# Closing steps of a threshold search taken between logits, and modulation steps moved to both ends of the attention stage

## What is computed

```python
mod = c_act @ w_ada[l] + b_ada[l]
sh1, sc1, gt1, sh2, sc2, gt2 = jnp.split(mod, 6)      # axis -1
h = rms_norm(x, g_pre_mix) * (1.0 + sc1) + sh1
qa, ka, va, cq, ckv, kidx, widx = split(h @ w_in)
out_a = sliding_window_sink_attention(qa, ka, va, ...)   # window of 2 chunks of 64
# group B, blocks of 128 queries:
score = einsum(w_idx, relu(q_idx . k_idx)); idx = top_k(score, 256)
logits over the kept keys - slopes * distance; softmax; times v
mix = concat(out_a, out_b) @ w_o
x = x + gt1 * rms_norm(mix, g_post_mix)
h2 = rms_norm(x, g_pre_ffn) * (1.0 + sc2) + sh2
x = x + gt2 * rms_norm((silu(gate) * up) @ w_down, g_post_ffn)
```

## Time and profile before

| what | value |
|---|---|
| median of 3 runs | 3391.96 us (3391.65 to 3392.4) |
| profiled execution, its own time | 3388.4 us |
| its span | 3386.6 us |
| TensorE busy over the span | 2987.1 us (88%) |
| VectorE busy | 1701.3 us (50%) |
| ScalarE busy | 1574.6 us (46%) |
| GpSimd busy | 318.4 us (9%) |

### The profile page before, as it was taken

One profiled execution on the slowest core, in us unless ns is written; L12 is line 12 of the kernel. 1 busy time (PEld: TensorE's weight loads), 2 busy tenths in 40 slices (PEclk: granted clock), 3 DMA queues, 4 the chain that ended last, 5 costly groups with the idle time before them and its releaser, 6 DMA issues. The chain is left out here.

```text
span 3386.6 us, 42835 instructions
## 1 busy us (share of the span) xinstructions
PE 2987.1 (88%) x14649; PEld 2439.3 (72%) x14649; DVE 1701.3 (50%) x3080; ACT 1574.6 (46%) x3023; POOL 318.4 (9%) x990
## 2 busy tenths in 40 slices
PE   5689888888878878778899699999999999999997
PEld 2467676666766666667788588788878887888876
DVE  2146677676776677765355344244432444244422
ACT  1357787767677577685433222232222322232222
POOL 0012222212121121020011000000000000000000
PEclk8688889888888888788899799999999999999999
DMA  5011110000000000000355433343323433343323
GB/s 208 15 45 38 47 32 29 23 26 26 16 14 26 22 8 9 4 5 4 122 170 155 130 99 93 118 138 98 99 87 123 143 93 99 111 143 99 94 92 106
DMA packets 316075, 254.86 MB, mean 75 GB/s; under 512 B 9153, under 2 KB 271905, under 8 KB 315809
## 3 DMA queue, kind: packets, MB, share of 16 engines
q1 hardware_dynamic: 282544, 236.29, 22.5%
q10 hardware_dynamic: 33392, 16.81, 1.7%
HBM read 219.50 MB, written 33.57 MB: 75 GB/s over the span
## 5 line engine op out<-in xcount | busy, mean ns | idle before, releaser
L1961 ACT ACTIVATE p_hi<-raw 128x1024 fp32r<-128x1024 f32 x264 | 279.3, 1058 | 693.8 <-PE dbank L1932 354.7
L2035 DVE TENSOR_TENSOR p_lo<-raw,p_hi 128x1024 fp32r<-128x1024 f32 x264 | 323.4, 1225 | 425.5 <-ACT p_hi L1961 425.4
L1115 ACT ACTIVATE logit<-tbank 128x512 f32<-128x512 f32 (+3 forms) x448 | 214.6, 488 | 288.5 <-PE tbank L851 286.5
L867 PE MATMUL obank<-vb,logit 128*128 128x64 f32 x2176 | 318.1, 294 | 0.0
L1289 DVE TENSOR_SCALAR_CACHE_REDUCE above<-score,cand 128x384 uint8<-128x384 f32 (+6 forms) x224 | 315.9, 1410 | 4.4
L1137 ACT ACTIVATE signs<-score,pick 128x512 int8<-128x512 f32 (+6 forms) x224 | 304.3, 1359 | 21.9 <-POOL pick L633 13.4
L867 PEld LDWEIGHTS obank<-vb,logit 128*128 128x128 f32 x2176 | 312.5, 219 | 0.0
L836 PE MATMUL lbank<-kb,qb_hi 128*128 128x512 f32 (+3 forms) x320 | 166.8, 521 | 156.5 <-DVE mx L1348 134.2
L1913 PE MATMUL gbank<-x_hi,p_hi 128*128 128x512 f32 x704 | 275.1, 391 | 29.3 <-DVE p_lo L2035 29.3
L1930 PE MATMUL dbank<-p_hi,a_hi 128*128 128x512 f32 x704 | 278.5, 396 | 17.0 <-DVE a_lo L2063 14.0
L851 PE MATMUL tbank<-ident,logit 128*128 128x128 f32 x1336 | 256.5, 307 | 36.6 <-ACT logit L1105 19.3
(11 more groups left out here) (219 smaller groups left out, 5280.5 us busy)
## 6 DMA issues: line engine op xcount, KB each, us to landing
raw<-in_w_gate_up SPq DMA_DIRECT2D x176, 512.0 KB, 3.8
raw<-in_w_down SPq DMA_DIRECT2D x88, 512.0 KB, 3.7
ada<-in_w_ada ACTq DMA_DIRECT2D x32, 512.0 KB, 3.8
wada<-in_w_ada SPq DMA_DIRECT2D x4, 2048.0 KB, 15.5
x_in<-in_x SPq DMA_DIRECT2D x16, 512.0 KB, 4.0
mixT<-oT SPq DMA_DIRECT2D x32, 256.0 KB, 2.3
mix<-mixT SPq DMA_DIRECT2D x16, 512.0 KB, 6.3
x_rows<-in_x SPq DMA_DIRECT2D x16, 512.0 KB, 4.6
```

The source lines that it names most:

```text
L867: mm = nc.tensor.matmul(obank[o % 2][:, h * HD:(h + 1) * HD], logit[:, i % 4, (4 * g + j) * P:(4 * g + j + 1) * P], v, start=(g == 0 and j ...
L1961: nc.scalar.activation(p_hi[:, s], raw[:, s], ACT.Copy).then_inc(panel_high, 1)
L2035: nc.vector.tensor_tensor(p_lo[:, s], raw[:, s], p_hi[:, s].bitcast(F32), ALU.subtract).then_inc(panel_ready, 1)
```

## The change

The search gets a third closing step, `bias` 0, which is what wrote `bias_b` at the end of `ties` 1. It stays behind the logits of head 7. `ties` 0 and `ties` 1 now take `between` and read logits behind their single instructions. `vector_weight` changes: in the iteration ahead of the block's companion heads, local heads 0 to 2 weigh 4.5 instead of 1.0 and local heads 4 to 7 weigh 3.0 instead of 4.0. The steps `mod` leave the local heads of all iterations. Six each stand behind local heads 0, 1, 2, 4, 6 and 7 of blocks 0 and 1 (before: two in block 1), the four behind companion head 5 of iterations 0 to 3 stay, and sixteen stand behind all companion heads of iterations 13 and 14. `mod_rows` moves from companion head 1 of iteration 14 to companion head 0 of iteration 15, and GpSimd's `modulate` from head 0 to head 4 there.

```diff
@@ -177,10 +177,10 @@
 
 
 
-SEARCH = [("bit", j) for j in range(32)] + [("ties", 0), ("ties", 1)]
+SEARCH = [("bit", j) for j in range(32)] + [("ties", 0), ("ties", 1), ("bias", 0)]
 
 ON_SCALAR = [("bit", j) for j in range(32)]
-AFTER_SCALAR = [("above", 0), ("ties", 0), ("ties", 1)]
+AFTER_SCALAR = [("above", 0), ("ties", 0), ("ties", 1), ("bias", 0)]
 
 
 def searched_by_scalar(b):
@@ -192,7 +192,7 @@
     it, kind, h = slot
     scoring = it + 2 < NB and h <= 3
     if kind == "A":
-        return (0.0 if it == b - 2 else 1.0) if scoring else 4.0
+        return (0.0 if it == b - 2 else 1.0 if h == 3 else 4.5) if scoring else 3.0
     room = 0.5 + 0.41 * (it + 1)
     if it + 3 < NB and h in (2, 4, 6):
         room -= 1.0
@@ -234,14 +234,14 @@
         wts = [scalar_weight(b, slot) for slot in slots[:-3]]
         for slot, r in zip(slots, spread(wts, len(ON_SCALAR))):
             scalar[slot] = [(b, ON_SCALAR[n]) for n in r]
-        for slot, action in zip(slots[-3:], AFTER_SCALAR):
-            vector[slot] = [(b, action)]
+        for slot, action in zip(slots[-3:] + slots[-1:], AFTER_SCALAR):
+            vector.setdefault(slot, []).append((b, action))
     else:
         wts = [vector_weight(b, slot) for slot in slots[:-2]]
-        for slot, r in zip(slots, spread(wts, len(SEARCH) - 2)):
+        for slot, r in zip(slots, spread(wts, len(SEARCH) - 3)):
             vector[slot] = [(b, SEARCH[n]) for n in r]
-        for slot, action in zip(slots[-2:], SEARCH[-2:]):
-            vector[slot] = [(b, action)]
+        for slot, action in zip(slots[-2:] + slots[-1:], SEARCH[-3:]):
+            vector.setdefault(slot, []).append((b, action))
     return vector, scalar
 
 
@@ -292,7 +292,7 @@
         for h in range(HEADS):
             steps.append(("head", "A", b, h, (), ()))
             front_a(b + 1, h)
-            if b and h in (1, 7):
+            if h in (0, 1, 2, 4, 6, 7):
                 modulate()
         steps += [("queries", "A", b + 1), ("gains", b + 1), ("latent", b + 1), ("latent_up", b + 1),
                   ("norm", b + 2)]
@@ -311,8 +311,6 @@
                 add(("scores", nxt, h + 1))
             if h == 2:
                 add(("queries", "B", b))
-            if h in (1, 7):
-                modulate()
         for h in range(HEADS):
             at = (b, "B", h)
             steps.append(("head", "B", b, h, tuple(vector.get(at, ())), tuple(scalar.get(at, ()))))
@@ -321,9 +319,9 @@
                       4: [("latent_up", b + 3)]}.get(h, []))
             if b + 4 < NB and h == 4:
                 add(("norm", b + 4))
-            if h == 5 and b < 4:
+            if (h == 5 and b < 4) or b in (NB - 3, NB - 2):
                 modulate()
-            if b == NB - 2 and h == 1:
+            if b == NB - 1 and h == 0:
                 add(("mod_rows",))
     return steps, beside
 
@@ -671,7 +669,7 @@
                     for b, action in s[5] + tuple(x for x in s[4] if x[1][0] == "above"):
                         move_pick(b, action)
                     shift()
-                if s[0:4] == ("head", "B", NB - 1, 0):
+                if s[0:4] == ("head", "B", NB - 1, 4):
                     modulate()
                 if s[0] not in ("norm", "gains"):
                     continue
@@ -1269,9 +1267,10 @@
                     threshold_bit(b, action[1], between)
                 elif action[0] == "above":
                     count_next(b, between)
+                elif action[0] == "ties":
+                    ties(b, action[1], between)
                 else:
-                    ties(b, action[1])
-                    between(3)
+                    mask_bias(b)
 
             def count_next(b, between):
 
@@ -1296,7 +1295,7 @@
                 link(nc.vector.scalar_tensor_tensor(cand[:], cand[:], following, reject[:],
                                                     ALU.bitwise_xor, ALU.bitwise_xor), between)
 
-            def ties(b, part):
+            def ties(b, part, between):
 
                 L = P * (b + 1)
                 thr = (pick if searched_by_scalar(b) else cand)[:].bitcast(F32)
@@ -1309,20 +1308,24 @@
                     else:
                         dve.wait_ge(lat_ssq, NB)
                     nc.vector.tensor_scalar(equal[:, 0:L], score[:, b % 2, 0:L], thr, None, ALU.is_equal)
+                    between(1)
 
                     link(nc.vector.tensor_scalar(above[:, 0:L], score[:, b % 2, 0:L], thr, None,
-                                                 ALU.is_lt, ALU.add, accum_out=count[:]))
+                                                 ALU.is_lt, ALU.add, accum_out=count[:]), between, 2)
                     link(nc.vector.tensor_tensor_scan(rank[:, 0:L], equal[:, 0:L], equal[:, 0:L], 0.0,
                                                       ALU.add, ALU.max))
 
                     link(nc.vector.scalar_tensor_tensor(need[:], rank[:, L - 1:L], float(TOPK - L), count[:],
-                                                        ALU.add, ALU.add))
+                                                        ALU.add, ALU.add), between)
                     return
                 link(nc.vector.scalar_tensor_tensor(equal[:, 0:L], rank[:, 0:L], need[:], equal[:, 0:L],
-                                                    ALU.is_gt, ALU.mult))
-
-                link(nc.vector.tensor_tensor(above[:, 0:L], above[:, 0:L], equal[:, 0:L], ALU.add))
-
+                                                    ALU.is_gt, ALU.mult), between, 1)
+
+                link(nc.vector.tensor_tensor(above[:, 0:L], above[:, 0:L], equal[:, 0:L], ALU.add), between)
+
+            def mask_bias(b):
+
+                L = P * (b + 1)
                 dve.wait_ge(piece_read, plan.last_piece("B", b - 1))
                 nc.vector.scalar_tensor_tensor(bias_b[:, 0:L], above[:, 0:L], -BIG, ndist[:, T - L:],
                                                ALU.mult, ALU.add).then_inc(bias_ready, 1)
@@ -1378,8 +1381,8 @@
             def head(i, kind, b, h, actions):
                 pieces = len(key_chunks(kind, b))
 
-                last = [x for x in actions if x[1] == ("ties", 1)]
-                actions = [x for x in actions if x[1] != ("ties", 1)]
+                last = [x for x in actions if x[1][0] == "bias"]
+                actions = [x for x in actions if x[1][0] != "bias"]
                 parts = pieces + 1
                 done = 0
```

## The result

The changed kernel takes 3343.36 us (median of 3335.3 to 3349.0), beside 3391.81 us of the kernel before on the same chip: a ratio of 0.986, 95% interval 0.9837 to 0.9883, or 48 us less. The forecast was 3372, with a range down to 3348. The sign was right; the gain is more than twice the forecast and outside the range.

What follows compares the result with a forecast made beforehand. No engine is full in the mixing stage, so the order within each engine's queue sets the time. The terms -36 - 30 + 36.5 + 14 - 4 = -19.5 us took 3392 to 3372 us, range 3348 to 3397.

Steps and rivals of the forecast that it cites:

- Part 3: Blocks 0 and 1: six modulations each wait in order for weight loads, +36.5 us, ends +26 and +42.
- Part 4: Companion heads of iterations 13 and 14: sixteen modulations placed there cost +14 us, ends 0 and +29.
- Rival A: TensorE's queue, blocks 0 and 1, iterations 13 and 14: modulation costs in full, +22 us, 3414; chance 0.20.
- part 5: Local heads 0 to 2: new weights move VectorE's bit steps there from crowded heads, -4 us, ends -15 and +10.
- part 1: Companion closings: logits read between closing steps use VectorE's idle time, -36 us, ends 0 and -57.
- the 60% of the ceiling: Share of the 51.7 us of VectorE idle time in the fourteen closings taken as won: 31 us.
- rival B: Closings: VectorE runs without a gap through heads 6 to 7, TensorE keeps its clock; -40 us, 3352; chance 0.13.
- part 2: Local heads of iterations 0 to 12: 26 modulations leave heads 1 and 7, -30 us, ends -27 and -48.
- The lower bound of part 2: Local heads 1 and 7: ScalarE's visible waits for the modulation product give 27 us at least.
- the three signs by which the forecast was to be wrong: Front costs under 30 us; late closings keep their length; iteration 14's heads grow by the full 1.84 us.
- Rival C: Closings of even blocks: moved steps lock out GpSimd, delaying ScalarE; +18 us, no change, 3390; chance 0.16.

Runs made afterwards that it cites:

- the two runs above: Kernel before with only head 1's thirteen modulation products 128 columns wide: 3349.61 us; kernel before with only head 1's thirteen steps moved to iterations 13 and 14: 3335.45 us.

## Why the prediction was wrong

**Part 3, the front: right.** +36.5 forecast, +38.8 measured, +39.0 with the modulations alone. The projection started where it was said, and the four waits for a load behind heads 0 to 2 were 3.49, 3.33, 2.94 and 2.69 us, as the loads' 3.8 less the heads between. An in-order wait behind a load can be counted from rows.

**Part 4, the back: right alone, too dear together.** +14 forecast, +13.9 measured for the modulations alone. With the closings interleaved as well, iterations 13 and 14 changed by -7.0 us where the closings alone gave -12.7, so the sixteen cost about 6. Rival A (whose 3414 leaves out part 5's 4 us) assumed the opposite, that interleaved closings would make each one show in full. It fell: TensorE's busy time rose by 10 us in each of the two iterations and their time did not follow; and part 1 gave more than the 39 us under which A was to decide.

**Part 5, the weights: nothing to be seen.** -4 forecast; the run alone shows +3, interval -2 to +7.

**Part 1, the closings: a term too small.** -36 forecast, -51 measured, inside its ends. The step that failed is "what is late next is TensorE, which has 16.3 us of work in the 21 us of iteration 12's window, so 4.7 of the 7.6 us is what it allows", and with it the 60% of the ceiling. VectorE's idle time in the windows fell from 52.7 to 6.0 us: nearly all of it went. Iterations 12 to 14 became 6.9, 7.8 and 10.1 us shorter, where the forecast had 4 to 6.

The 16.3 us were taken as an amount of work that has to fit into the window. They weren't that, for two reasons. They were busy time at a clock of 0.76, partly an effect of the waiting that the change removes. And TensorE's part in the window is not fixed: in iteration 12 it went down from 128 records to 99, and the clock was lower too, 0.73 after 0.81. The rows up to the bias, before and with the closings interleaved:

```profile
1348.10:1375.30 27.20, 20.82 (x128) 18.61 (x126) 19.52 (x28) 9.59 (x19) 0.00 (x0) 0.81 0.01 2
...
1309.10:1329.40 20.30, 17.90 (x99) 15.74 (x97) 19.05 (x28) 9.39 (x18) 0.00 (x0) 0.73 0.00 0
```

In iteration 14, whose closing before held 23.07 us of TensorE's busy time at 0.72, the interleaved one has 16.20 us at full clock for nearly the same number of records (128 and 125):

```profile
1550.90:1581.30 30.40, 23.07 (x128) 21.25 (x127) 20.70 (x27) 11.64 (x18) 0.00 (x0) 0.72 0.00 1
```

```profile
1500.30:1520.60 20.30, 16.20 (x125) 14.70 (x123) 20.05 (x26) 8.70 (x14) 0.00 (x0) 1.00 0.00 1
```

VectorE then runs without a gap (20.05 of 20.30), which is the ceiling of rival B. So B was near on the size of this term (-57 against -51), and its reason, "TensorE keeps its clock", holds for iterations 13 and 14 but not for 12. B's 3352 was still above the result, since it left part 2 as it was.

**Part 2, the modulations out of the heads: the term that broke the range.** -30 forecast, with -48 as the end; 59 us measured. The end was thought to be hard, 26 products of 1.84 us, "if TensorE were the limit everywhere". The assumption in it was that a removed step takes only its own duration along. Behind ten of the thirteen at head 1, what followed ran at half clock for some us. In block 13 that is, beside the step's own 1.84 us, 2.06 us for the 22 value products, 0.85 us for the queries (3.72 to 2.87), and the rest in the score products. Over the thirteen it is 37 us on top of their own 24, by the two runs above. Head 7's set, moved alone, gave 23.7 - 13.0 = 11 us between front and back, and nothing that can be seen on top of head 1's 61: both together gave 59. The trace of before had the sign of it. The clock of block 12's local heads stood at 0.67, block 13's at 0.70, and the forecast had read TensorE's clock only in the closings and in the front, never behind a `mod` of the middle.

The lower bound of part 2, read from ScalarE's wait for `mod_cols`, did not price the clock either: that wait ends with the product, and the loss begins there. None of the three signs by which the forecast was to be wrong came up; none of them looks at the clock or at the local heads.

**Rival C** had the wait right and the price wrong. In the changed kernel ScalarE waits 12.3 us for GpSimd's `pick` in iterations 0 to 12, where it was 6.1:

```profile
ACT signs L1135 <- POOL pick L631: 12.3, 17, 1.8
```

That is 6 us more, not 18, and the kernel was faster all the same. Behind it, in iteration 13, the wait fell from 6.1 to 4.1 us. The Trainium skill (SBUF — State Buffer, section Who interferes with whom) names such a lock between VectorE and GpSimd; these 6 us are what this case shows at most, and no run here parts the lock from other reasons for a late `pick`.

## What to carry to other kernels

Before an end is called hard, look at the granted clock of the stretch in which the step stands: busy time at 0.7 of the clock is not an amount of work, and a step that lowers the clock takes more along with it than its own length. If narrow products have to stand among others, writing them wider by repeating a column is worth one run; here it gave 37 us with one edited line. And a serial step (product, copy, load into the same buffer) costs its whole round trip wherever the heads between are short, so it belongs among long ones.

## What the runs showed of the hardware

Sixteen float32 products of one column each, 1.95 us together, behind the scores of local head 1, were followed by TensorE at half clock in block 13: 4.63 us for 22 products that take 2.57 otherwise. Ten of thirteen such places had a clock of 0.50 to 0.68 in the 5 us behind, three had 1.00. The same sixteen at 128 columns took 2.05 us and the clock stayed at 1.00. The same one-column products among projections did no such thing. Timeline of TensorE in the changed kernel, block 0 around head 4:

```profile
127.86 3.65 PE L731 MATMUL work<-w_in,h_T 128*128 128x512 f32 x8
131.35 1.84 PE L789 MATMUL work<-c_act,ada 128*128 128x1 f32 x16
...
133.62 3.65 PE L731 MATMUL work<-w_in,h_T 128*128 128x512 f32 x8
```

Eight projection records take 3.65 us ahead of the products and 3.65 us behind them, so the surroundings count. What else in them decides was not tried.
